# A hybrid decoder step on one core: the expert rows of five output tiles are gathered in two parts

## The reference

```
g_w, g_idx = top_k(softmax(xt @ w_rg + b_rg), 1)       # one of 8 groups
e_w, e_idx = top_k(softmax(logits of that group), 2)   # two of its 8 experts
weights    = g_w * e_w / sum(e_w)
y[token]   = sum over the two experts of weights * (silu(x @ w_gate[e]) * (x @ w_up[e])) @ w_down[e]
out        = rmsnorm(x + y, norm_f_g)                  # x is called x2 in the kernel
```

## Time and profile before

| | us |
|---|---|
| median of 3 runs | 2040.82 |
| lowest and highest | 2031.3, 2046.83 |
| the profiled execution | 2023.4 |
| its span | 2021.6 |
| PE busy in the span | 1857.5 |
| DVE, ACT, POOL busy | 598.3, 426.5, 301.4 |

### The profile page before, as it was taken

How to read it: one execution, slowest core, us unless ns; L and a number is a source line. 1 busy time by engine, 2 the same in 40 slices (tenths; PEclk the granted TensorE clock), 3 DMA queues, 4 the chain that set the end, 5 groups by cost and what they waited for, 6 DMA issues and landing times. The chain is left out here.

```text
span 2021.6 us, 26766 instructions
## 1 busy us (share of the span) xinstructions
PE 1857.5 (92%) x10622; PEld 1088.8 (54%) x10622; DVE 598.3 (30%) x1385; ACT 426.5 (21%) x904; POOL 301.4 (15%) x428
## 2 busy tenths in 40 slices
PE   7999999999999999998999998999598988888884
PEld 5644444444445656565666664555365555555551
DVE  3110000022203334333555554555322211111116
ACT  3211111100002223332444333222110011101103
POOL 1021221111100000000111112243412111111100
PEclk9999999999999999998999998999598889999997
DMA  7212211378820000024999996454599999999986
GB/s 232 107 68 80 75 36 70 116 261 284 276 86 1 1 1 1 1 63 128 292 305 292 294 304 224 148 185 162 192 400 421 420 416 416 415 402 403 407 342 260
DMA packets 105267, 433.86 MB, mean 215 GB/s; under 512 B 24208, under 2 KB 29808, under 8 KB 74384
## 3 DMA queue, kind: packets, MB, share of 16 engines
q1 hardware_dynamic: 84880, 331.06, 43.5%
q0 software_dynamic: 20160, 101.24, 15.0%
q10 hardware_dynamic: 128, 0.20, 0.0%
HBM read 389.22 MB, written 63.66 MB: 224 GB/s over the span
## 5 line engine op out<-in xcount | busy, mean ns | idle before, releaser
L838 PE MATMUL psum<-arena 128*128 128x512 f32 (+1 forms) x1280 | 527.3, 567 | 0.0
L838 PEld LDWEIGHTS psum<-arena 128*128 128x128 f32 x1280 | 239.6, 190 | 259.7 <-issue 235.7
L1266 PE MATMUL psum<-arena 128*64 128x256 f32 (+1 forms) x2048 | 284.4, 411 | 66.4 <-DMA arena<-in_w_up_dram 65.5
L1266 PEld LDWEIGHTS psum<-arena 128*64 128x64 f32 (+1 forms) x2048 | 204.8, 155 | 136.2 <-issue 79.2
L1285 PE MATMUL psum<-arena 128*64 128x512 f32 (+1 forms) x512 | 131.4, 595 | 0.7 <-DVE arena L2223 0.7
L1896 DVE COPY arena<-psum 128x512 f32<-128x512 f32 (+5 forms) x52 | 27.8, 545 | 346.9 <-PE psum L883 194.0
L1033 PEld LDWEIGHTS psum<-arena 128*128 128x128 f32 x1024 | 112.7, 141 | 30.0 <-issue 28.0
L1435 ACT ACTIVATE arena<-psum 128x512 f32<-128x512 f32 (+1 forms) x72 | 40.5, 562 | 412.6 <-PE psum L838 400.0
L1033 PE MATMUL psum<-arena 128*128 128x128 f32 x1024 | 126.6, 276 | 0.3 <-DVE arena L1950 0.3
L1163 PE MATMUL psum<-arena 128*128 128x512 f32 x256 | 113.4, 600 | 1.3 <-ACT arena L1484 1.3
L2219 DVE TENSOR_TENSOR arena<-arena,psum 128x256 f32<-128x256 f32 x36 | 15.2, 422 | 321.4 <-ACT arena L1549 321.4
(11 more groups left out here) (307 smaller groups left out, 1949.8 us busy)
## 6 DMA issues: line engine op xcount, KB each, us to landing
arena<-in_w_gate_dram SPq DMA_DIRECT2D x64, 1024.0 KB, 13.3
arena<-in_w_up_dram SPq DMA_DIRECT2D x64, 1024.0 KB, 20.1
arena<-in_w_down_dram SPq DMA_DIRECT2D x64, 1024.0 KB, 21.8
arena<-in_w_in_dram SPq DMA_DIRECT2D x8, 2048.0 KB, 8.2
z_act<-arena SPq DMA_DIRECT2D x64, 256.0 KB
rope_turned<-arena SPq DMA_DIRECT2D x32, 512.0 KB
arena<-rope_turned SPq DMA_DIRECT2D x64, 256.0 KB
arena<-z_act SPq DMA_DIRECT2D x8, 2048.0 KB, 10.1
```

Source lines behind the costliest of these rows:

```text
L838: last = mm(out[:, 0:w], xn_t[:, k, t * P:t * P + P], w_blk[n % 2][:, k, 0:w], start=(k == 0), stop=(k == KD - 1))
L1266: last = mm(bank(2 + u)[rows, DE * x:DE * x + DE], xg_t[u][:, k, rows], w_e[slot][x][:, k, :], start=(k == 0), stop=(k == KD - 1))
```

## The change

`PE_TILES` becomes (1, 3, 5, 7). The rows of tiles 1, 3, 5, 6 and 7 (`EARLY_TILES`) are no longer loaded by SP behind `moe_end`, but gathered by POOL in two parts, each with two indirect DMAs per tile (one per choice, 128 rows of 4 KB): the first part during the last steps, behind the scatter of step 33 (`n_late`), with an index list in which the rows of the last three steps' experts are out of bounds and so skipped; the second behind `moe_end`, with the complementary list. DVE computes the lists in pieces 10 to 14 of `overflow`. The early tiles lie in slots 0 and 1 and over `xg`, so the first part waits until gate and up of step 34 are done and all rows are turned. Tiles 0, 2, 4 and 8 are loaded by SP as before. `y_rows` is filled once with the inputs, early, so that a skipped or not yet written row is defined. The diagonals are built ahead of the wait on `moe_end`, and the overflow loop uses slots 2 and 3.

```diff
--- before.py
+++ after.py
@@ -62,7 +62,10 @@
 CAPR = (TOK + BLK - 1) // BLK * BLK
 NBLK = NE * CAPR // P
 PAD = 1e6
-PE_TILES = (2, 4, 6)
+PE_TILES = (1, 3, 5, 7)
+EARLY_TILES = (1, 3, 5, 6, 7)
+PLAIN_TILES = (0, 2, 4, 8)
+LATE_STEPS = 3
 FIRST_ROPE = 40
 CAP_STEPS = (TOK + BLK - 1) // BLK - 1
 QB = 2 * H * P
@@ -429,12 +432,22 @@
         slot_in, slot_f = prod_all[:, 0:2 * P], prod_all[:, 2 * P:4 * P]
         fill = w_uk_t.rearrange("p h c -> p (h c)")[:, 0:2 * NE * CAPR // P]
 
-        o = [attn_base]
-        y2 = [take(2 * D, o) for _ in range(NT)]
+        slot_at = [attn_base + 6 * D * s for s in range(4)]
+        y_home = {1: slot_at[0], 3: slot_at[0] + 2 * D, 5: slot_at[1], 7: slot_at[1] + 2 * D, 6: attn_base + 26 * D,
+                  0: slot_at[0] + 4 * D, 2: slot_at[1] + 4 * D, 4: slot_at[2], 8: slot_at[2] + 2 * D}
+        y2 = [take(2 * D, [y_home[t]]) for t in range(NT)]
         fin = [x[:, 0:D] for x in y2]
+        o = [slot_at[3]]
         junk8 = take(D, o)
         stat8 = [take(2, o) for _ in range(NT)]
-        diag = {t: [take(P, o) for _ in range(2)] for t in PE_TILES}
+        assert o[0] <= attn_base + 4 * 6144
+        o = [gains_base + 4 * D]
+        kept_in = take(2 * NT * NE, o).rearrange("p (m e) -> p m e", e=NE)
+        limit, is_late, row_f, row_at = (take(2 * NT, o) for _ in range(4))
+        early_i, late_i = (take(2 * NT, o).bitcast(U32) for _ in range(2))
+        assert o[0] <= free[0]
+        diag = {t: [kept_in.rearrange("p m e -> p (m e)")[:, 2 * P * k + P * c:2 * P * k + P * c + P] for c in range(2)]
+                for k, t in enumerate(PE_TILES)}
         assert o[0] <= attn_base + 4 * 6144
 
 
...
@@ -563,6 +577,18 @@
                 return [(dst[:, c, 2 * n + x], src[:, x, c]) for x in range(2) for c in range(2)]
             src = out[0:DR, 0:H * RS].rearrange("p (h b t) -> p h b t", h=H, b=NB)
             return [(qsr[half, :].rearrange("p (b h t) -> p h b t", b=NB, h=H), src) for half in (slice(0, DR), slice(DR, P))]
+
+        def y_there(eng, t):
+
+            if t in PLAIN_TILES:
+                eng.wait_ge(f_in[PLAIN_TILES.index(t)], 16)
+            else:
+                k = EARLY_TILES.index(t)
+                eng.wait_ge(c_in[k % 4], cache_moves(k % 4) + 32 * (k // 4 + 1))
+
+        def cache_moves(q):
+
+            return 16 * (NCH // 4) + (16 * PRE if q < 2 else 0)
 
         def row_sum(t):
 
@@ -661,6 +687,11 @@
             sp.wait_ge(rows_stored, 64)
 
 
+            sp.wait_ge(fill_in, 16)
+            for c in range(2):
+                sp.dma_start(y_rows[TOK * c:TOK * c + SEQ, :], xp).then_inc(fill_in, 16)
+                sp.dma_start(y_rows[TOK * c + SEQ:TOK * c + TOK, :], xs).then_inc(fill_in, 16)
+
             def rope_load(n):
                 if n >= 4:
                     sp.wait_ge(c_s, n - 3)
@@ -769,8 +800,8 @@
                         e0 = sp.value_load(ovf_id[0:1, bass.ds(2 * j, 1)], min_val=0, max_val=NE - 1)
                         e1 = sp.value_load(ovf_id[0:1, bass.ds(2 * j + 1, 1)], min_val=0, max_val=NE - 1)
                         sp.wait_ge(e_y[1], NST + j)
-                        w_load(0, e0)
-                        w_load(1, e1)
+                        w_load(2, e0)
+                        w_load(3, e1)
 
 
             def out_rows(sp, t):
@@ -779,14 +810,10 @@
 
             sp.wait_ge(moe_end, 1)
             yr = y_rows.rearrange("(n c) d -> n (c d)", c=2)
+            for k, t in enumerate(PLAIN_TILES):
+                r = rows_of(t)
+                sp.dma_start(y2[t][0:r, :], yr[t * P:t * P + r, :]).then_inc(f_in[k], 16)
             for t in range(NT):
-                r = rows_of(t)
-                if t >= 4:
-                    sp.wait_ge(f_in[t % 4], 16 * (t // 4))
-                sp.dma_start(y2[t][0:r, :], yr[t * P:t * P + r, :]).then_inc(f_in[t % 4], 16)
-                if t >= 6:
-                    out_rows(sp, t - 6)
-            for t in range(3, NT):
                 out_rows(sp, t)
             sp.wait_ge(f_st, 16 * NT)
 
...
@@ -1313,7 +1340,7 @@
             pe.wait_ge(moe_end, 1)
             pe.wait_ge(r_dve, NT + 3)
             for k, t in enumerate(PE_TILES):
-                pe.wait_ge(f_in[t % 4], 16 * (t // 4 + 1))
+                y_there(pe, t)
                 for half in range(2):
                     cols = slice(512 * half, 512 * half + 512)
                     mm(bank(2 * k + half), ident, x2[:, t, cols], start=True, stop=False)
@@ -1769,20 +1796,35 @@
                 pool.sem_inc(yo_free[s], 1)
 
             row_of = [row for row, _ in steps]
+            pool.wait_ge(fill_in, 80)
             for n in range(4):
                 rows_in(n, row_of[n], n)
             for n in range(2):
                 pool.wait_ge(e_xt, n + 1)
                 rows_in(n, row_of[n + 4], n + 4)
             k = 6
+            def y_gather(t, c, rows_i, done):
+                m = 2 * t + c
+                pool.indirect_dma_start(y2[t][:, D * c:D * c + D], None, y_rows, bass.IndirectOffsetOnAxis(ap=rows_i[:, m:m + 1], axis=0),
+                                        bounds_check=last_slot, oob_is_err=False).then_inc(done, 16)
+
+            n_late = NST - LATE_STEPS
             for n in range(NST):
-                if n >= 2:
+                if 2 <= n and n - 2 != n_late - 1:
                     scattered((n - 2) % 4, (n - 2) // 4 + 1)
                 rows_out(n % 4, n, row_of[n], k)
                 k += 1
                 if n + 6 < NST:
                     rows_in((n + 2) % 4, row_of[n + 6], k)
                     k += 1
+                if n == n_late:
+                    scattered((n_late - 1) % 4, (n_late - 1) // 4 + 1)
+                    pool.wait_ge(e_gu, NST - 1)
+                    pool.wait_ge(e_xt, NST)
+                    pool.wait_ge(rows_split, 1)
+                    for t in EARLY_TILES:
+                        for c in range(2):
+                            y_gather(t, c, early_i, e_x[1])
             for n in range(NST - 2, NST):
                 scattered(n % 4, n // 4 + 1)
             pool.wait_ge(slots_ok, 3)
@@ -1804,6 +1846,12 @@
                         rows_out(0, NST + j, NST, 2 * NST + 4 * j + 3)
                         scattered(0, j + yo_used + 1)
             pool.sem_inc(moe_end, 1)
+            pool.wait_ge(e_x[1], 16 * len([n for n in range(NST) if n % 4 == 1]) + 32 * len(EARLY_TILES))
+            for k, t in enumerate(EARLY_TILES):
+                if k >= 4:
+                    pool.wait_ge(c_in[k % 4], cache_moves(k % 4) + 32 * (k // 4))
+                for c in range(2):
+                    y_gather(t, c, late_i, c_in[k % 4])
 
 
             pool.wait_ge(late_in, 16)
@@ -2208,6 +2256,30 @@
                     tt(g_sub, logits[:, :, 0:NG], g_top[:, :, 0:1].broadcast_to([P, NT, NG]), ALU.subtract)
                     step(tt(d_sub, e_top[:, :, 1], e_top[:, :, 0], ALU.subtract))
                     dve.sem_inc(r_sub, 1)
+                elif k == 10:
+                    late_e = [r for _, mine in steps[NST - LATE_STEPS:] for r, _, _ in mine]
+                    assert late_e == list(range(late_e[0], late_e[-1] + 1))
+                    cap, used, past = cnt[1], cnt[2], cnt[3]
+                    ts(cap, placed, float(NBIG), float(BLK), ALU.is_lt, ALU.mult)
+                    ts(used, placed, float(late_e[0]), None, ALU.is_lt)
+                    step(ts(past, placed, float(late_e[-1] + 1), None, ALU.is_ge))
+                    step(tt(used, used, past, ALU.add))
+                    step(stt(cap, cap, float(BLK), used, ALU.add, ALU.mult))
+                elif k == 11:
+                    step(tt(kept_in, iota.unsqueeze(1).broadcast_to([P, 2 * NT, NE]), wide(e_f.rearrange("p t c -> p (t c)"), NE), ALU.is_equal))
+                elif k == 12:
+                    step(tt(kept_in, kept_in, cnt[1].unsqueeze(1).broadcast_to([P, 2 * NT, NE]), ALU.mult))
+                elif k == 13:
+                    step(red(limit, kept_in, AX.X, ALU.add))
+                elif k == 14:
+                    tt(is_late, rk.rearrange("p t c -> p (t c)"), limit, ALU.is_ge)
+                    step(copy(row_f, ids_sb.rearrange("p (n c) -> p n c", c=2)[:, :, 0]))
+                    step(stt(row_at, is_late, float(1 << 20), row_f, ALU.mult, ALU.add))
+                    step(copy(early_i, row_at))
+                    step(ts(is_late, is_late, -float(1 << 20), float(1 << 20), ALU.mult, ALU.add))
+                    step(tt(row_at, is_late, row_f, ALU.add))
+                    step(copy(late_i, row_at))
+                    dve.sem_inc(rows_split, 1)
 
 
             def rows_t(n, u):
@@ -2258,11 +2330,11 @@
             step(tt(g_den, g_den, d_sub, ALU.mult))
             step(V.reciprocal(gates[:, :, 0], g_den))
             step(tt(gates[:, :, 1], gates[:, :, 0], d_exp, ALU.mult))
-            dve.wait_ge(moe_end, 1)
             for t in PE_TILES:
                 for c in range(2):
```

(6 more changed lines are left out.)

## The result

The changed kernel takes 2040.06 us in the median of 20 runs (2032.78 to 2046.38), the kernel before 2030.4 in 20 (2024.11 to 2046.83): ratio 1.0045, interval 1.0033 to 1.0058, that is 9.1 us slower. That is inside the 1% that was called no difference. The forecast of 2042 lies close to the time, but by luck: it stood on a three-run median that was 10.4 us above that of 20 runs, and the forecast step was +1.1 us where +9.1 was measured, so that 8 us too few hid 10 us too many.

A forecast was written before the change was run, and what follows sets the result against it. Weights on the DMA engines bound the expert stage; behind it, the last landing, then TensorE and VectorE. A landing 2.1 us later and a longer first-tile wait, less saved work, gave +1.1 us: 2024.5 profiled, 2042 median; range 2031 to 2050.

The forecast's parts named there:

- The fill: Four DRAM-to-DRAM copies into y_rows during the attention stage: 46 us at 376 GB/s, fully covered, cost 0.
- VectorE's lists: Index-list preparation on VectorE in steps 13 to 17: some 6.5 us, covered while TensorE waits for weights, cost 0.
- step one: POOL's queue before experts_done: early gathers drain at 1982.9, so the last scatter lands at 1983.9 instead of 1981.8, +2.1 us.
- The 3 us of slack of the down weights: Step 35: down weights land at 1971.1, TensorE's product behind them at 1974.1, so 3 us of delay would be free.
- rival B: POOL's queue, 1963 to 1982: early gathers starve the last scatter; 2044.5 and up to 2052 us, chance 0.14.
- the +4.7 of 286 GB/s: Slow bound for the last scatter: early gathers at 286 GB/s take 22.3 us, landing at 1986.5, +4.7 us.
- B's own sign: What would show rival B in the trace: a last landing over 5 us.
- step two: Behind experts_done: tile 1's late gather lands in 6.5 us, between 3.4 and 9.5, so tile 1 is there at 1992.8.
- Rival A: Behind experts_done: late rows come at once and the queue drains in time; -4.0 us, 2036.8 us, chance 0.28.
- Rival C: In the tail: VectorE operations with two SBUF inputs keep POOL from writing descriptors; +8.2 us, 2049 us, chance 0.07.
- Rival D: Early/late split fails, almost all rows count as late, ten full gathers follow experts_done; about +1 us, 2042, chance 0.03.

The follow-up runs named there:

- e3: The changed kernel without the early gathers; the ten gathers behind experts_done fetch all rows: ratio 1.0026 to the kernel before.
- e1: The changed kernel run again, unaltered: ratio 1.0021 to the kernel before.
- e2: The changed kernel with 128 semaphore increments put into ScalarE's instruction list ahead of the expert steps: ratio 1.0039 to the kernel before.
- e5: The changed kernel with SP's loads of tiles 2, 4 and 8 held back until tile 1's late rows have landed: ratio 1.0013 to the kernel before.
- e7: The changed kernel without the ten late gathers, so 32 rows are missing from the sums: ratio 1.0004 to the kernel before.
- e6: The changed kernel with three tiles (1, 3, 6) gathered early instead of five, SP loading tiles 5 and 7 whole: ratio 1.0023 to the kernel before.
- e10: The changed kernel run a third time, unaltered, next to e9 on the same chip: ratio 1.0043 to the kernel before.
- e9: The changed kernel with both the three early tiles of e6 and the held-back SP loads of e5: ratio 0.9972 to the kernel before.

## Why the prediction was right and wrong

**Right.** No difference by 1%, and why the work saved doesn't show: VectorE's chain begins behind TensorE's first tile. From its scaling to the end 18.7 + 2.4 = 21.1 us were forecast, 21.05 came. The fill is hidden: its last copy, issued at 607.4, lands 26.7 us later, so the whole takes 28.6 us where 46 were worked out, and SP's next transfer is at 896.9:

```profile
605.45 0.62 SPq L692 DMA_DIRECT2D y_rows<-in_x_prompt_dram  x1
...
896.87 1.75 SPq L701 DMA_DIRECT2D arena<-rope_turned  x4
```

So are the diagonals and VectorE's lists (e3). The bulk of the early gathers was to drain 19.7 us after their start, 21.0 behind the scatter of step 33, and was over at 18.9. POOL's gathers came at the forecast pace (1.30 us each).

**Wrong, step one: "it lands at 1983.9 instead of 1981.8, +2.1 us".** Measured +5.1 to +5.5 (e1, e2, e5, e7) and, with ScalarE's pause, +7.2 (changed). The drain was worked out from total bytes by a mean rate, which gives the end of the bulk (forecast at 21.0 us, measured at 18.9). What counts is the end of the trail, 5 us later. The trace before had it, though none of the rows quoted: weights whose queue was nearly empty at 1968 landed at 1971.1. The 3 us of slack of the down weights were used up too (10.4 to 14.4 us under way), but that ran beside the queue, as the prediction had it: e7 lands no earlier without it. The mechanism of rival B, the queue ahead of the last scatter, is what happened; e6 shows it. It came by a trail and not by a low rate, and the landing is 0.4 to 0.8 us beyond the +4.7 of 286 GB/s. In the changed kernel's first trace and in e10 B's own sign, a late landing, is absent (2.39 and 2.40 us), because the pause, which nobody forecast, holds the scatter back for longer than the trail lasts.

**Wrong, step two: "I take 6.5" for tile 1's late gather.** It took 9.3 to 9.9, the upper end (9.5), which came from the median beside weights. SP's 3.3 MB are issued within 2 us of the first load and the second gather 2.1 us after it (1.3 was assumed), so it meets the whole backlog. The argument that they had just started pointed the other way than it was used. e5 and e9, with one load beside the gathers, show the lower end (3.2 and 2.7 against 3.4). In the changed kernel the gather is 3.3 us longer than taken and issued 0.8 us later, and with TensorE's first tile at 7.8 us instead of 7.3 this makes the tail 3.7 longer where 1.0 shorter was forecast. The rule of turns between queues in the Trainium skill ("DMA: Bandwidth & Descriptors", queues, rings and completion order) would have let a gather of eight descriptors per engine pass after one packet; the trace doesn't agree, with 9.84 us beside SP's loads.

**Rival A** needed what e5 and e9 had to provide by holding SP back. **Rival C** had a real hold at a wrong price. Late gathers were written while VectorE ran scalar_tensor_tensor with two SBUF tensors, first in the changed kernel, then in e3:

```profile
2004.11 1.15 POOL L1808 DMA_INDIRECT arena<-y_rows,arena  x1 [0.30 <-issue]
...
2004.44 1.28 DVE L2351 SCALAR_TENSOR_TENSOR arena<-arena 128x1024 f32<-128x1024 f32 x1
...
2006.89 0.99 POOL L1808 DMA_INDIRECT arena<-y_rows,arena  x1 [0.30 <-issue]
```

```profile
1991.06 1.28 DVE L2346 SCALAR_TENSOR_TENSOR arena<-arena 128x1024 f32<-128x1024 f32 x1 [0.77 <-DMA arena<-y_rows]
...
1991.45 1.75 POOL L1808 DMA_INDIRECT arena<-y_rows,arena  x1 [0.30 <-issue]
```

The gather of e3 starts early in an operation and takes 1.75 us. It is done 0.86 us after that operation ended. The one at 2004.11 takes 1.15 us, again done 0.86 us after the end (2004.40) of the operation that ran at its start; the scatter in the earlier trace rows is done 0.89 us after it. The one at 2006.89 starts when such an operation is all but over and takes 0.99. So the hold lasts for what is left of one operation, and the next one, though it follows at once, adds nothing. With operations of 1.28 us that is 0.2 us in the changed kernel and 0.8 in e3. Rival C had the gathers wait for a pause of VectorE, which gave its 8.2 us. **Rival D** is out: the late parts were small, as e5's landing of 3.16 us against e3's 12.6 for full ones shows.

## What to carry to other kernels

A transfer moved into an idle stretch must be through, to its last packet, before the next thing that everybody waits for enters the same queue; total bytes by mean rate is not that time, and the last landings in the trace before tell the difference. Small transfers on which the chain hangs go first: here holding back SP's loads behind the first until two small gathers had landed was worth 6 to 8 us of tail (e5, e9), more than the 3 to 4 us of tail that moving the rows early gave. And a bound that a row gives for just this situation (a gather beside loads) should be taken as the value, not averaged with the idle case.

## What the runs showed of the hardware that was not expected

- The copy of 8.65 MB within DRAM took 28.6 us from its first issue to its last landing: 302 GB/s read and as much written, while the SP queue moves 376 GB/s in the mean of the run.
- The second of two gathers of 128 rows, nearly all skipped: 2.7 to 3.2 us beside one load of 1 MB (e9, e5), 9.3 to 9.9 beside 3.3 MB of SP's loads (changed, e1, e2, e10).
- Behind ten gathers the last scatter landed 25.0 to 25.4 us after that of step 33, whether it was issued at 19.2 or at 20.8 (e1, e2, e5, e7).
- A TensorE wait of 1.75 us was followed by sums of 5.35 instead of 3.7 us and a clock of 0.72 over them (e1), waits of 1.88 and 1.57 us were not (3.66 us at 1.00; e2, e9).
- A VectorE operation with two SBUF tensors holds POOL's indirect DMA until the one operation has ended: 2.32 us under a tensor_tensor of 2.42, 1.75 (e3) and 1.15 under scalar_tensor_tensors of 1.28, 0.99 to 1.03 with no hold.
- Releases 2 to 6 us late with no named source in three of eight traces with early gathers; open.
